# Delta rule: 64-step inverses from two blocks of 32 on 32x32 tiles of TensorE and a third from products; routing order and out-projection rewritten

## The chip, the cores and the metric

One core of one Trainium2 chip runs the whole program. The metric is the device time of one execution in microseconds, for fixed inputs. Everything is float32.

## The reference, cut to what matters

The program is one block of a bidirectional mixer model (neighbourhood attention, gated linear attention and a delta rule, whose outputs are concatenated and projected), followed by two layers of attention or a gated recurrence, each with a mixture of experts. 1024 tokens of width 1024 with 64 meta tokens ahead in the first block; 16 experts, each of which picks the 128 tokens it likes best.

```
# delta rule, per head (width 64) and per direction: state S, inputs r, decay w, k, v, a, b
S = S * w + (S @ a) b^T + v k^T ;  y = S @ r
# block one out
h = x + concat(o_na, o_gla, o_rw) @ w_out[0]
h = h * rsqrt(mean(h*h) + 1e-6) * final_norm_g
# expert choice
aff = softmax(x @ w_router);  gates, idx = top_k(aff^T, 128)
out[idx] += (silu(x[idx] @ gate) * (x[idx] @ up)) @ down * gates
```

The kernel computes the delta rule in chunks of 64 steps. Within a chunk it needs the inverse T = (I - A)^-1 of a unit triangular 64x64 matrix, A being strictly triangular. The doubling form is used: T = (I + A)(I + A^2)(I + A^4)..., for 64 steps up to A^32.

## The kernel before, in words

Each engine has its own instruction stream, written out by hand in Python (functions `..._tensor`, `..._vector`, `..._scalar`, `..._gpsimd`, and `sync` for the transfers), and each instruction waits for counters that the other engines' instructions raise. There is no planner: the order in each stream is the order of the calls.

**Delta rule** (`rwkv_branch`, 842 to 1612 us of the span). Eight heads are done as four pairs p of heads h = 0, 1. A pair has 17 chunks for each direction d = 0, 1. They are done in five groups: q = 0 with one chunk (the meta tokens), q = 1 to 4 with four chunks. A group G = 5p + q works in lane G % 2, which has three PSUM banks (`bank[0..2]`) and a strip of SBUF. So in a full group there are 2 heads x 4 chunks x 2 directions = 16 small problems side by side: direction d lies on partitions `B_(d)` (64 of them), the heads and chunks beside each other along the free axis. A product over a full group is 16 matmuls 64x64x64; as float32 each matmul gives two records (two passes) in the profile.

The steps of a group are: `scores_tensor` (A and the scores, masked by `masks_vector`), `powers_tensor` (A transposed, masked by `powers_vector`), `a_tensor`, `kb_tensor`, `v_turn_tensor` (transposes, copied by `front_scalar`), the levels, `akv_tensor`, `wu_tensor` (T times two right sides), `qpd_tensor` (matrices of the chunk's step), and `chain_tensor`, four dependent steps of the state.

A level e = 0 to 5 of the inverse (`level_tensor`, L1553 on) makes M = A^(2^(e+1)) in bank 0 (L1563, e < 5), its transpose MT in bank 1 (L1568, e < 4) and T's next term TT in bank 2 (L1578, e > 0). `m_scalar` (L1813) and `mt_scalar` (L1818) copy M and MT to SBUF on ScalarE, `mt1_vector` (L1981) copies the first MT on VectorE, `tt_vector` (L1986) adds the TT product to T on VectorE. GpSimd makes T = A + I at the start (`group_gpsimd`, L1354). So a full group has 5 + 4 + 5 = 14 level products.

TensorE's stream interleaves groups: levels 0, 1, 2 of G stand between level 5, akv, wu and qpd of G - 1; then come level 3 of G, scores and powers of G + 1 with chain steps of G - 1 between them, level 4 of G, and the transposes of G + 1. Between two pairs (`between_tensor`, and likewise on the other engines) the last group's levels 3 to 5, wu, qpd and chain stand among the wide projections of the next pair (L1402) and its low-rank products (L1423).

**Out-projection of block one** (`block_one_out`, 1612 to 1799.5). Eight tiles of 128 tokens. The SP queue loads the scale vector, the first tile's 12 source blocks (768 KB), a tile of x and then the weights in six transfers of 1 MB. `out_products` takes tile after tile: 12 blocks x 2 halves of 512 columns. VectorE adds x to both halves, ScalarE squares 1024 columns with a sum, VectorE scales and shifts, ScalarE takes the root, VectorE the reciprocal, and VectorE writes X.

**Routing** (`moe`, once per layer: 2285.5 to 2355.6 and 3566 to 3635.4). In turn k TensorE makes the logits of tile k - 1 (L3127), turns tile k of X (L3134), turns the logits of tile k - 1 (L3141), and spreads expert 0's column of tile k - 2 over a bank (L3108, `spread_tensor`). ScalarE copies X's transpose (L3228) and the logits (L3231), then takes the exponential of tile k - 1 (L3235). VectorE takes the maximum, normalizes (L3375, L3377), copies the transposed affinities (L3381) and counts, for each token of expert 0, how many are ahead of it (`count_vector`, L3324), reading the spread row from PSUM banks 6 and 7. Each spread waits until all counts of the tile before are done:

```
pe.wait_ge(counted.sem, counts_to[k - 2])
spread_tensor(pe, 0, k - 2)
```

When all 8 tiles are counted, the 128 tokens of expert 0 are listed (L3354, L3114), fetched by an indirect transfer and turned (L3160), and the experts' products begin (L3174), whose weights stream through a ring of 24 slabs of 512 KB.

The functions of the delta rule and the routing that the change touches, and their callers:

Of the kernel before, what the change touches and what calls it, by code (L numbers as in the profile page):

```python
# [13 lines left out]
P = 128  # L14
# [1171 lines left out]
def rwkv_branch(k, c, ps, io, hnT, mix, sb):  # L1186
# [5 lines left out]

    nc = k.nc
    with stage(k, sb) as st:
        PAIRS, GROUPS, FULL = 4, 5, 4
# [32 lines left out]
            "m_made", "m_copied", "mt_made", "mt1_copied", "mt_copied", "tt_made", "tt_added"))  # L1228
        akv_made, akv_copied, w_made, w_copied, u_made, u0_copied, u1_copied = (st.sem(n) for n in (
# [8 lines left out]
        class Lane:  # L1238


            def __init__(self, G):
# [11 lines left out]
                self.M, self.MT = (tall(0), tall(1)), (None, tall(4), tall(5), tall(4), tall(5))  # L1253
# [4 lines left out]
            def tall(self, i):  # L1258
                return self.bank[i][:, 0:2 * self.n * CH].rearrange("p (h c t) -> p h c t", h=2, t=CH)

# [65 lines left out]
        def prepare_gpsimd(gp, p):  # L1326
# [7 lines left out]
            for t in edges[0:4 if p else 8]:  # L1334
                gp.memset(t, 0.0).then_inc(*padded.up())
            for d, excl in enumerate((excl0, excl1)):
                gp.wait_ge(summed.sem, 3 * p + 1 + 2 * d)
                gp.tensor_tensor(excl, temps(p)[0][2 * d + 1], excl, ALU.subtract).then_inc(*excluded.up())
# [11 lines left out]
        def group_gpsimd(gp, G):  # L1350
            L = Lane(G)
            gp.wait_ge(masked.sem, 4 * G + 4)
            for d in range(2):
                gp.tensor_tensor(L.TT[B_(d)], L.SC[B_(d), d, :, :, sa],  # L1354
                                 eye[B_(d), :].unsqueeze(1).unsqueeze(1).broadcast_to([CH, 2, L.n, CH]),
                                 ALU.add).then_inc(*eyed.up())

        def gpsimd(gp):
            for p in range(PAIRS):
                prepare_gpsimd(gp, p)  # L1360
                for q in range(GROUPS):
                    group_gpsimd(gp, GROUPS * p + q)

# [179 lines left out]
        def m0_t(L, d, h, i):  # L1543
            return L.SC[B_(d), d, h, i, sa]

        def level_tensor(pe, G, e):
# [5 lines left out]
            else:  # L1552
                pe.wait_ge(m_copied.sem, 5 * G + e)  # L1553
                if e == 1:
                    pe.wait_ge(mt1_copied.sem, G + 1)
                elif e < 5:
                    pe.wait_ge(mt_copied.sem, 3 * G + e - 1)
            power = lambda d, h, i: L.M[e % 2][B_(d), h, i, :]
            power_t = lambda d, h, i: m0_t(L, d, h, i) if e == 0 else L.MT[e][B_(d), h, i, :]
# [5 lines left out]
            if e < 4:  # L1565
                for h, i in L.units():
                    for d in range(2):
                        x = pe.matmul(L.tall(1)[B_(d), h, i, :], power(d, h, i), power_t(d, h, i))  # L1568
                x.then_inc(*mt_made.up())
            if e:  # L1570
                if e == 1:
                    pe.wait_ge(eyed.sem, 2 * G + 2)
                    pe.wait_ge(akv_copied.sem, G + 1)
                else:
                    pe.wait_ge(tt_added.sem, 5 * G + e - 1)
                for h, i in L.units():
                    for d in range(2):
                        x = pe.matmul(L.tall(2)[B_(d), h, i, :], power(d, h, i), L.TT[B_(d), h, i, :])  # L1578
                x.then_inc(*tt_made.up())

# [73 lines left out]
        def between_tensor(pe, p):  # L1654

            G, old, new = GROUPS * p - 1, p > 0, p < PAIRS
            if old:
# [8 lines left out]
                chain_tensor(pe, G - 1, 2)  # L1666
            if new:
                k_tensor(pe, p, 0)
            if old:
                chain_tensor(pe, G - 1, 3)  # L1670
                level_tensor(pe, G, 5)
# [31 lines left out]
        def tensor(pe):  # L1703
            for i in range(2):
                block_tensor(pe, i, ps[3 * i:3 * i + 3], enumerate(SPANS))
            for p in range(PAIRS):
# [13 lines left out]
                for q in range(GROUPS):  # L1720
                    G = GROUPS * p + q
                    level_tensor(pe, G, 0)
                    if q:
                        level_tensor(pe, G - 1, 5)
# [31 lines left out]
                    if q >= 2:  # L1756
                        chain_tensor(pe, G - 1, 3)
                    v_turn_tensor(pe, G + 1)
# [51 lines left out]
        def m_scalar(ac, G, e):  # L1810
            L = Lane(G)
            ac.wait_ge(m_made.sem, 5 * G + e)
            ac.activation(L.M[e % 2], L.tall(0), ACT.Copy).then_inc(*m_copied.up())  # L1813

        def mt_scalar(ac, G, e):
            L = Lane(G)
            ac.wait_ge(mt_made.sem, 4 * G + e)
            ac.activation(L.MT[e], L.tall(1), ACT.Copy).then_inc(*mt_copied.up())  # L1818
# [1863 lines left out]
```

## Time and profile before

| | us |
|---|---|
| median of 3 runs | 4355.24 (4348.53 to 4356.75) |
| the profiled execution's own time | 4353.24 |
| its span | 4351.5 |
| TensorE busy (matmuls) | 4065.1 (93%) |
| VectorE, ScalarE, GpSimd busy | 1542.3, 1050.6, 288.7 |
| delta rule | 770, TensorE busy 726.9 |
| out-projection of block one | 187.5, TensorE busy 167.8 |
| routing, first and second layer | 70.1 and 69.4, TensorE busy 41.8 and 42.2 |

How to read it: the profile records every instruction of each engine. A matmul record's start is measured; its length contains the pipeline, so records of one product overlap and the distance of starts is what a product costs. "Idle before, releaser" is the time an engine stood still ahead of an instruction and whose semaphore ended it.

### The profile page before, as it was taken

To read this page: it belongs to the slowest core of one execution; us is meant where nothing else is said; L and a number is where in the kernel's file an instruction comes from. 1 tells how busy PE (TensorE), PEld (TensorE's weight loads), DVE (VectorE), ACT (ScalarE), POOL (GpSimd) and SP (SyncE) were. 2 spreads that over 40 slices of the span, in tenths; PEclk is the share of its full clock that TensorE was granted. 3 is DMA by queue.
4 is the path that set the end of the run, shared out by engine and by line. 5 is a ranking of instruction groups with operands and counts; after the bars stand their busy time and mean duration, and the time that the engine had idled before them with its cause. 6 is when DMAs were issued, how large, how long until landed. Compare 5 with 4: busy or idle time off the path is not lost. (4 is left out here: it accounts for less than half of the span.)

```text
span 4351.5 us, 65830 instructions
## 1 busy us (share of the span) xinstructions
PE 4065.1 (93%) x28648; PEld 2292.5 (53%) x28648; DVE 1542.3 (35%) x3438; ACT 1050.6 (24%) x2064; POOL 288.7 (7%) x350
## 2 busy tenths in 40 slices
PE   7999898999999979999997999999899887999998
PEld 4555575596868664554544444444444344444443
DVE  2344233435454531124655411112345627211113
ACT  2233221343333320104552000002234421000002
POOL 0000000101110100000110000000000110000000
PEclk9999899999999989999998999999999988999999
DMA  3000101100000013112007899998311126899997
GB/s 96 25 25 6 46 16 45 30 4 26 3 26 8 7 58 111 49 20 49 1 1 283 294 323 310 326 306 306 113 38 34 48 105 253 300 307 328 309 324 253
DMA packets 319470, 566.70 MB, mean 130 GB/s; under 512 B 47776, under 2 KB 127808, under 8 KB 319184
## 3 DMA queue, kind: packets, MB, share of 16 engines
q1 hardware_dynamic: 305296, 511.12, 34.7%
q0 software_dynamic: 9504, 34.61, 3.3%
q10 hardware_dynamic: 4384, 16.78, 1.0%
q8 instruction: 226, 3.70, 0.3%
q14 instruction: 60, 0.49, 0.0%
HBM read 514.20 MB, written 48.23 MB: 129 GB/s over the span
## 5 line engine op out<-in xcount | busy, mean ns | idle before, releaser
L3174 PE MATMUL bank<-ring,m_picked_T 128*128 128x512 f32 x2048 | 898.4, 597 | 4.1 <-ACT m_picked_T L3250 4.1
L3174 PEld LDWEIGHTS bank<-ring,m_picked_T 128*128 128x128 f32 x2048 | 389.3, 192 | 482.2 <-issue 476.6
L3174 PE MATMUL bank<-ring,m_hidden_T 128*128 128x512 f32 x1024 | 454.7, 592 | 0.0
L3174 PEld LDWEIGHTS bank<-ring,m_hidden_T 128*128 128x128 f32 x1024 | 189.8, 190 | 216.3 <-issue 216.3
L1402 PE MATMUL bank<-hnT,w_block 128*128 128x336 f32 (+3 forms) x800 | 270.9, 488 | 18.1 <-DMA w_block<-in_w_in 18.1
L376 PE MATMUL bank<-hnT,w_block 128*128 128x512 f32 (+3 forms) x640 | 248.2, 523 | 5.1 <-DMA w_block<-in_w_in 5.1
L3416 DVE TENSOR_TENSOR m_hidden<-m_hidden,bank 128x512 f32<-128x512 f32 x64 | 43.9, 686 | 522.0 <-ACT m_hidden L3256 522.0
L232 PE MATMUL bank<-xT,w_block 128*128 128x512 f32 x512 | 220.5, 592 | 1.0 <-DMA w_block<-in_lru_w_in 1.0
L1402 PEld LDWEIGHTS bank<-hnT,w_block 128*128 128x128 f32 x800 | 149.0, 192 | 106.6 <-issue 22.7
L2241 PE MATMUL bank<-out_w,out_in 128*128 128x512 f32 x384 | 167.8, 600 | 18.6 <-DMA out_w<-in_w_out 18.6
L3256 ACT ACTIVATE m_hidden<-bank 128x512 f32<-128x512 f32 x64 | 38.2, 597 | 540.1 <-PE bank L3174 540.0
L232 PEld LDWEIGHTS bank<-xT,w_block 128*128 128x128 f32 x512 | 97.2, 190 | 123.2 <-issue 122.0
L376 PEld LDWEIGHTS bank<-hnT,w_block 128*128 128x128 f32 x640 | 114.4, 192 | 77.7 <-issue 44.7
L2459 PE MATMUL bank<-xT,a_weights 128*128 128x512 f32 x320 | 140.5, 592 | 0.8 <-ACT xT L2340 0.8
L2241 PEld LDWEIGHTS bank<-out_w,out_in 128*128 128x128 f32 x384 | 74.0, 193 | 112.5 <-issue 112.5
L2814 PE MATMUL bank<-l_xc,l_wg 128*128 128x512 f32 x256 | 112.9, 602 | 19.4 <-ACT l_r L2880 17.0
L2520 PE MATMUL bank<-a_weights,xT 128*128 128x512 f32 x256 | 124.9, 615 | 0.4 <-ACT xT L2557 0.4
L3422 DVE COPY m_hidden_T<-bank 128x256 f32<-128x256 f32 x64 | 27.0, 422 | 273.9 <-PE bank L3167 273.9
L3547 POOL DMA_INDIRECT y_rows<-m_ys,m_tokens x30 | 47.7, 1589 | 1108.4 <-DVE m_ys L3431 1047.6
L3260 ACT ACTIVATE m_hidden_T<-bank 128x256 f32<-128x256 f32 x64 | 24.5, 383 | 393.3 <-PE bank L3167 393.3
L808 PE MATMUL bank<-hnT,w_block 128*128 128x512 f32 (+3 forms) x288 | 113.2, 550 | 0.0
L1986 DVE TENSOR_TENSOR rw_lane<-bank,rw_lane 128x512 f32<-128x512 f32 (+1 forms) x100 | 61.0, 610 | 145.1 <-PE bank L1578 145.1
(480 smaller groups left out, 5697.2 us busy)
## 6 DMA issues: line engine op xcount, KB each, us to landing
ring<-in_moe_w_gate_up SPq DMA_DIRECT2D x512, 512.0 KB, 7.6
ring<-in_moe_w_down SPq DMA_DIRECT2D x256, 512.0 KB, 4.6
w_block<-in_w_in SPq DMA_DIRECT2D x42, 512.0 KB, 3.8
x_rows<-X ACTq DMA_DIRECT2D x2, 4096.0 KB, 16.4
ring<-y_rows SPq DMA_DIRECT2D x16, 512.0 KB, 8.7
w_block<-in_lru_w_in SPq DMA_DIRECT2D x16, 512.0 KB, 3.9
out_in<-mix SPq DMA_DIRECT2D x8, 768.0 KB, 5.9
out_w<-in_w_out SPq DMA_DIRECT2D x6, 1024.0 KB, 13.4
```

The costliest lines, as they stand in the source:

```text
L232: m = pe.matmul(ps[banks + j][0:out_rows, 0:n], w[:, d, 0:out_rows], src[:, d, col:col + n], start=d == 0, stop=d == KD - 1)
L376: x = pe.matmul(bank_of(s + j)[:, 0:w], wb[b % RING][:, d, :], hnT[:, d, col:col + w], start=d == 0, stop=d == KD - 1)
L808: x = pe.matmul(bank(kind, p, j, h)[:, 0:n], wb[i % 3][:, d, :], hnT[:, d, col:col + n], start=d == 0, stop=d == KD - 1)
L1402: m = pe.matmul(banks[j][:, 0:n], wb[i % 3][:, d, :], hnT[:, d, col:col + n], start=d == 0, stop=d == KD - 1)
L1986: ve.tensor_tensor(L.part(2), L.bank[2][:, 0:2 * L.n * CH], L.part(2), ALU.add).then_inc(*tt_added.up())
L2241: m = pe.matmul(ps[2 * u + h][:, :], xt[u][:, b, :], wt[:, b, 512 * h:512 * h + 512], start=b == 0, stop=b == blocks - 1)
L2459: x = pe.matmul(ps[m % 4][:, :], w, xT[:, d, 512 * (m % 2):512 * (m % 2) + 512], start=d == 0, stop=d == KD - 1)
L2520: x = pe.matmul(ps[6 + half][:, :], oT[:, b, t * P:(t + 1) * P], weights[:, b, 512 * half:512 * half + 512], start=b == 0, stop=b == KD - 1)
L2814: out = pe.matmul(ps[s % 4][:, :], wg[:, q, z, h, x * P:(x + 1) * P], xc[:, h, col:col + w], start=h == 0, stop=h == 1)
L3174: m = pe.matmul(banks[j][:, :], lhsT[:, (i % 8) * P:(i % 8 + 1) * P], ring[:, i, j, :], start=i % 8 == 0, stop=i % 8 == KD - 1)
L3416: ve.tensor_tensor(hid[:, s], hid[:, s], ps[2 * h][:, :], ALU.mult).then_inc(*acted.up())
L3547: gp.indirect_dma_start(y_rows[:, :], bass.IndirectOffsetOnAxis(ap=tokens[:, e:e + 1], axis=0), ys[:, :], None, compute_op=ALU.add).then_i ...
```

## The change

**Delta rule.** A 64-step chunk is split into two blocks of HC = 32 steps. The diagonal blocks of T are inverted by doubling up to A^16, which needs one level less, on 32 of the partitions each, so that the two blocks of the two directions lie on four different 32x32 tiles of TensorE (`block(d, j)` gives the rows and columns of block j). A level product is now 32 matmuls 32x32x32 (64 records) in place of 16 of 64x64x64 (32 records); M is made in levels 0 to 3, MT in 0 to 2, TT in 1 to 4. The block off the diagonal is T2 * A21 * T1: `between_blocks_tensor` turns T1 ("back") and multiplies A21 with T2 ("cross"), ScalarE and VectorE copy the results, and `corner_tensor`, in the place of level 5, multiplies the two. GpSimd clears the zero corner of T and copies the diagonal blocks from their own tile TD to T (`place_gpsimd`); ScalarE and VectorE copy the corner. ScalarE's copies of v stand in a function of their own behind the copy of "back".

**Out-projection.** The first four tiles are done together, block by block: each block of weights (now 12 transfers of 512 KB on ScalarE's queue) and of sources (12 of 256 KB on SP's) is used as it lands. From tile 4 on it is tile after tile, one half after the other. The square is taken by halves, and the root by Ln and Exp.

**Routing.** In each turn ScalarE takes the exponential of tile k - 1 ahead of the logits' copy of tile k, and copies the spread row of tile k - 1 from PSUM to SBUF (`row0`); VectorE counts from there, and the spread waits for ScalarE's copy three turns back in place of the counts.

```
-        PAIRS, GROUPS, FULL = 4, 5, 4
+        PAIRS, GROUPS, FULL, HC = 4, 5, 4, 32
+            def block(self, d, j):
+                k = 1 - j if d and self.q else j
+                return slice(CH * (1 - d) + HC * k, CH * (1 - d) + HC * k + HC), slice(HC * k, HC * k + HC)
 # group_gpsimd, and behind it in the loop place_gpsimd of the group before
-                gp.tensor_tensor(L.TT[B_(d)], L.SC[B_(d), d, :, :, sa], eye..., ALU.add).then_inc(*eyed.up())
+                for j in range(2):
+                    rows, cols = L.block(d, j)
+                    gp.tensor_tensor(L.TD[rows], L.SC[rows, d, :, :, sa][:, :, :, cols],
+                                     eye[rows, cols].unsqueeze(1).unsqueeze(1).broadcast_to([HC, 2, L.n, HC]),
+                                     ALU.add).then_inc(*eyed.up())
+            for d in range(2):
+                gp.memset(L.TT[L.block(d, 1)[0]][:, :, :, L.block(d, 0)[1]], 0.0).then_inc(*tt_cleared.up())
+        def place_gpsimd(gp, G):
+            L = Lane(G)
+            gp.wait_ge(tt_added.sem, 4 * G + 4)
+            for d in range(2):
+                for j in range(2):
+                    rows, cols = L.block(d, j)
+                    gp.tensor_copy(L.TT[rows][:, :, :, cols], L.TD[rows]).then_inc(*tt_placed.up())
+            gp.wait_ge(*tt_placed.now())
 # level_tensor
-            if e < 5:
-                for h, i in L.units():
-                    for d in range(2):
-                        x = pe.matmul(L.tall(0)[B_(d), h, i, :], power_t(d, h, i), power(d, h, i))
+            blocks = [(h, i, d, j) for h, i in L.units() for d in range(2) for j in range(2)]
+            if e < 4:
+                for h, i, d, j in blocks:
+                    x = pe.matmul(L.half(0)[L.block(d, j)[0], h, i, :], power_t(h, i, d, j), power(h, i, d, j))
 ...
+        def between_blocks_tensor(pe, G):
+            pe.wait_ge(tt_added.sem, 4 * G + 4)
+            for h, i in L.units():
+                for d in range(2):
+                    first = L.block(d, 0)[0]
+                    x = pe.matmul(L.half(1)[side(d), h, i, :], L.TD[first, h, i, :], c["ident"][first, first])
+            x.then_inc(*back_made.up())
+            for h, i in L.units():
+                for d in range(2):
+                    second = L.block(d, 1)[0]
+                    x = pe.matmul(L.half(0)[side(d), h, i, :], L.M[0][second, h, i, L.block(d, 0)[1]], L.TD[second, h, i, :])
+            x.then_inc(*cross_made.up())
+        def corner_tensor(pe, G):
+            pe.wait_ge(back_copied.sem, G + 1)
+            pe.wait_ge(cross_copied.sem, G + 1)
+            for h, i in L.units():
+                for d in range(2):
+                    x = pe.matmul(L.half(2)[L.block(d, 0)[0], h, i, :], L.back[side(d), h, i, :], L.cross[side(d), h, i, :])
+            x.then_inc(*corner_made.up())
 # wu_tensor
-            pe.wait_ge(tt_added.sem, 5 * G + 5)
+            pe.wait_ge(tt_placed.sem, 4 * G + 4)
+            pe.wait_ge(tt_cleared.sem, 2 * G + 2)
+            pe.wait_ge(corner0.sem, G + 1)
+            pe.wait_ge(corner1.sem, G + 1)
 # tensor, in the loop over q
-                        level_tensor(pe, G - 1, 5)
+                        corner_tensor(pe, G - 1)
 ...
                     if q >= 2:
                         chain_tensor(pe, G - 1, 3)
+                    between_blocks_tensor(pe, G)
                     v_turn_tensor(pe, G + 1)
 # block_one_out
+            for b in range(BLOCKS):
+                pe.wait_ge(mix_in[b].sem, 16)
+                pe.wait_ge(w_in[b].sem, 16)
+                for t in range(TOGETHER):
+                    for h in range(2):
+                        m = product(t, h, b)
 # moe, tensor
-                    else:
-                        pe.wait_ge(counted.sem, counts_to[k - 2])
+                    elif k >= 4:
+                        pe.wait_ge(row_in.sem, k - 3)
 # moe, scalar: the exponential stands ahead of the logits' copy, and at the end of a turn
+                if k >= 1:
+                    ac.wait_ge(spread[0].sem, k)
+                    ac.activation(row0[:, (k - 1) * P:k * P], spread_bank(0, k - 1), ACT.Copy).then_inc(*row_in.up())
```

## Rows read from the trace of the kernel before

**Rows 1.** The page's engines, stretches by stage (busy per engine), the instruction queue.

```profile
PE 4065.1 (93%) x28648; PEld 2292.5 (53%) x28648; DVE 1542.3 (35%) x3438; ACT 1050.6 (24%) x2064; POOL 288.7 (7%) x350
...
842.00:1612.00 770.00, 726.92 (x15011) 579.40 (x15009) 366.33 (x665) 262.34 (x471) 88.72 (x79) 0.99 0.04 12
1612.00:1799.50 187.50, 167.80 (x384) 73.96 (x384) 23.77 (x41) 12.10 (x25) 0.00 (x0) 0.95 0.29 95
2285.50:2355.60 70.10, 41.78 (x251) 31.09 (x251) 35.72 (x210) 14.63 (x44) 1.47 (x4) 0.74 0.66 248
...
q8 instruction: 226, 3.70, 0.3%
```

**Rows 2.** Stretches: one steady group of the delta rule, columns as before.

```profile
911.97:940.27 28.30, 27.75 (x856) 26.48 (x852) 13.07 (x29) 9.43 (x17) 2.53 (x2) 1.00 0.01 3
```

**Rows 3.** TensorE in order of time inside that group: start, length, line, idle before.

```profile
914.76 1.16 PE L1500 MATMUL bank<-rw_ar,rw_kb 64*128 64x128 f32 x16 [0.49 <-DVE rw_lane L1967]
...
916.83 1.10 PE L1563 MATMUL bank<-rw_lane 64*64 64x64 f32 x32
917.76 1.10 PE L1578 MATMUL bank<-rw_lane 64*64 64x64 f32 x32
918.70 0.40 PE L1648 MATMUL bank<-rw_state,rw_lane 64*64 64x64 f32 x8
918.93 0.40 PE L1651 MATMUL bank<-rw_lane,rw_state 64*64 64x64 f32 x8
919.26 1.09 PE L1522 MATMUL bank<-ident,rw_ar 128*64 128x128 f32 x16
...
922.57 1.15 PE L1563 MATMUL bank<-rw_lane 64*64 64x64 f32 x32
923.55 1.10 PE L1568 MATMUL bank<-rw_lane 64*64 64x64 f32 x32
```

**Rows 4.** TensorE in order of time where akv meets level 1; four short records.

```profile
926.06 0.22 PE L1563 MATMUL bank<-rw_lane 64*64 64x64 f32 x1
926.07 0.22 PE L1586 MATMUL bank<-rw_lane 64*64 64x64 f32 x1
...
926.13 0.28 PE L1563 MATMUL bank<-rw_lane 64*64 64x64 f32 x3
...
322.79 0.24 PE L425 MATMUL bank<-na_k,na_q 64*64 64x16 f32 x4
```

**Rows 5.** VectorE and GpSimd in order of time, steady group and between two pairs.

```profile
909.38 0.76 DVE L2005 TENSOR_TENSOR rw_lane<-bank,rw_dec 128x256 f32<-128x256 f32 x2 [1.13 <-PE bank L1630]
...
917.77 0.47 DVE L2021 SCALAR_TENSOR_TENSOR rw_state<-bank,rw_dec,rw_lane 128x64 f32<-128x64 f32 x2
...
917.34 2.61 POOL L1354 TENSOR_TENSOR rw_lane<-rw_lane,rw_eye 64x512 f32<-64x512 f32 x2 [24.47 <-DVE rw_lane L1967]
...
1202.73 0.76 DVE L1997 TENSOR_TENSOR rw_lane<-bank,rw_ar 128x256 f32<-128x256 f32 x2 [5.65 <-PE bank L1609]
```

**Rows 6.** Out-projection in order of time, and a transfer of 512 KB.

```profile
1615.44 0.33 SPq L2265 DMA_DIRECT2D final_g<-in_final_norm_g  x1
...
1626.60 23.60 PE L2241 MATMUL bank<-out_w,out_in 128*128 128x512 f32 x48 [18.63 <-DMA out_w<-in_w_out]
...
1764.63 29.77 PE L2241 MATMUL bank<-out_w,out_in 128*128 128x512 f32 x69
...
1794.44 1.29 DVE L2285 TENSOR_TENSOR h_tile<-bank,h_in 128x512 f32<-128x512 f32 x2 [16.19 <-PE bank L2241]
...
w_block<-in_w_in SPq DMA_DIRECT2D x42, 512.0 KB, 3.8
```

**Rows 7.** Routing in order of time, TensorE and ScalarE.

```profile
2307.04 1.09 PE L3134 MATMUL bank<-ident,X 128*128 128x128 f32 x8 [1.25 <-DVE m_aff L3381]
...
2333.14 0.45 PE L3108 MATMUL bank<-ident,m_aff_tiles 128*128 128x128 f32 x1 [3.60 <-DVE m_junk L3324]
...
2305.82 0.27 ACT L3231 ACTIVATE m_logits<-bank 16x128 f32<-16x128 f32 x1 [2.09 <-PE bank L3127]
```

More of the change, by code:

```diff
@@ L1571, in level_tensor, with side @@
                 if e == 1:
-                    pe.wait_ge(eyed.sem, 2 * G + 2)
+                    pe.wait_ge(eyed.sem, 4 * G + 4)
                     pe.wait_ge(akv_copied.sem, G + 1)
                 else:
[L1575 to L1578, printed above, removed]
+                    pe.wait_ge(tt_added.sem, 4 * G + e - 1)
+                for h, i, d, j in blocks:
+                    rows = L.block(d, j)[0]
+                    x = pe.matmul(L.half(2)[rows, h, i, :], power(h, i, d, j), L.TD[rows, h, i, :])
                 x.then_inc(*tt_made.up())
+        def side(d):
+            return slice(HC * (1 - d), HC * (1 - d) + HC)
+        def between_blocks_tensor(pe, G):
+            L = Lane(G)
+            pe.wait_ge(tt_added.sem, 4 * G + 4)
[10 more added lines that the diff above has]
+        def corner_tensor(pe, G):
+            L = Lane(G)
+            pe.wait_ge(back_copied.sem, G + 1)
[4 more added lines that the diff above has]
+            x.then_inc(*corner_made.up())
         def akv_tensor(pe, G):
@@ L2269, in sync, with product @@
                     "(k p) e -> p k e", p=P)).then_inc(*k.router_in.up(16))
+            for t in range(TOGETHER, NT):
+                if t >= TOGETHER + 2:
+                    sp.wait_ge(made.sem, 2 * (t - 1))
+                sp.dma_start(xt[t % 2][:, :, :],
+                             mix[0:BLOCKS, :, t * P:(t + 1) * P].rearrange("b p t -> p b t")).then_inc(*src_in[t % 2].up(16))
+                x_tile(t)
             sp.wait_ge(*k.router_in.now())
         def tensor(pe):
-            out_products(pe, ps, blocks, wt, xt, src_in, w_in, used, taken)
+            def product(t, h, b):
+                src = first[:, b, t * P:(t + 1) * P] if t < TOGETHER else xt[t % 2][:, b, :]
+                return pe.matmul(ps[2 * (t % 4) + h][:, :], src, wt[:, b, 512 * h:512 * h + 512], start=b == 0,
+                                 stop=b == BLOCKS - 1)
@@ new lines, in tensor @@
+            for b in range(BLOCKS):
+                pe.wait_ge(mix_in[b].sem, 16)
[3 more added lines that the diff above has]
+                        m = product(t, h, b)
+                        if b == BLOCKS - 1:
+                            m.then_inc(*made.up())
+            for t in range(TOGETHER, NT):
+                pe.wait_ge(src_in[t % 2].sem, 16 * (t // 2 - 1))
+                for h in range(2):
+                    pe.wait_ge(added.sem, 2 * (t - 4) + h + 1)
+                    for b in range(BLOCKS):
+                        m = product(t, h, b)
+                    m.then_inc(*made.up())
@@ L2302, in block_one_out @@
+                ac.wait_ge(totalled.sem, t + 1)
+                ac.activation(s[:, 2:3], s[:, 2:3], ACT.Ln, bias=eps[:, :], scale=1.0 / D).then_inc(*logged.up())
+                ac.wait_ge(*logged.now())
+                ac.activation(s[:, 3:4], s[:, 2:3], ACT.Exp, scale=-0.5).then_inc(*rooted.up())
+        nc.gpsimd.memset(eps[:, :], 1e-6).then_inc(*eps_set.up())
         sync(nc.sync)
         tensor(nc.tensor)
+        scalar(nc.scalar)
         vector(nc.vector)
-        scalar(nc.scalar)
@@ L3103, in spread_bank @@
         def spread_bank(x, t):
-            return ps[(6, 2)[x] + t // 4][:, t % 4 * P:t % 4 * P + P]
+            return ps[2 + t // 4][:, t % 4 * P:t % 4 * P + P] if x else ps[6 + t % 2][:, 0:P]
         def spread_tensor(pe, x, t):
@@ L3323, in count_vector @@
                 ve.wait_ge(counted.sem, counted.n - 3)
+            row = ps[2 + first // 4][:, first % 4 * P:first % 4 * P + n * P] if x else row0[:, first * P:last * P]
             ve.scalar_tensor_tensor(junk[counted.n % 4][:, 0:n * P].rearrange("p (k j) -> p k j", j=P),
-                                    ps[(6, 2)[x] + first // 4][:, first % 4 * P:first % 4 * P + n * P].rearrange(
-                                        "p (k j) -> p k j", j=P), aff[:, t, x:x + 1],
+                                    row.rearrange("p (k j) -> p k j", j=P), aff[:, t, x:x + 1],
                                     weight[:, :].unsqueeze(1).broadcast_to([P, n, P]), op, ALU.mult,
@@ L3381, in vector @@
                     ve.tensor_copy(affT[:, t * P:t * P + P], ps[2 * (t % 3)][0:NE, 0:P]).then_inc(*aff_taken.up())
-                    ve.wait_ge(spread[0].sem, t + 1)
+                    ve.wait_ge(row_in.sem, t + 1)
                     count_before_vector(ve, 0, t)
```

179 lines of the change are left out of this document (116 added, 63 removed).

## Prediction

> **What bounds the kernel now.** First the share of busy time by engine and by stage [rows 1]: TensorE works 4065 of 4351.5 us. The change touches four places. In the delta rule (842 to 1612 us) TensorE is busy 726.9 of 770 us, VectorE 366, ScalarE 262. The out-projection (1612 to 1799.5) is TensorE's too, with 18.6 us of wait ahead of it. In the routing of the first expert layer (2285.5 to 2355.6; the second is alike) it is busy 60% and waits for VectorE. Then one steady group of the delta rule [rows 2]: it repeats every 28.30 us, TensorE busy in 27.75, VectorE in 13.1, ScalarE in 9.4, GpSimd in 2.5. So in a group TensorE's time is the time. The order of its instructions [rows 3] shows no gap but 0.49 us for a mask.
>
> **What one product costs.** A product over a full group is 16 matmuls, 32 records. L1563 starts at 916.83, L1578 at 917.76: 0.93 us, or 58 ns for each round of two records, one in each of two 64x64 tiles [rows 3]. In L2241 69 records of 512 columns take 29.77 us; without the last one's 0.60 that is 0.429 us each, 0.84 ns a column [rows 6]. 64 columns are 53 ns, so a round carries 5 ns besides. The new product is 32 matmuls of 32 columns, 64 records on four tiles. If four run side by side, a round is 27 + 5 = 32 ns, and 16 rounds take 0.51 us. That four can run side by side is seen where L1586 (off the diagonal) meets L1563 (on it): seven starts between 926.06 and 926.13, of which the first two and the last group stand in [rows 4], so four different tiles share one round of 58 ns. No row has 32x32 tiles. From below: four records of 16 columns end 0.24 us after the first starts and last 0.19, so two rounds start within 0.05, about 29 ns a round, 0.46 us a product [rows 4]. From above: if only two records share a round of 32 ns, 32 rounds, 1.01 us. I take 0.51, since the row nearest in kind shows four tiles. The three off-diagonal products (back, cross, corner: 32 records on two tiles) are 16 rounds too, 0.51 each.
>
> **A change of tile form.** From 64x64 to 128x64, L1651's eight records from 918.93 would be through at 919.16, the next form starts at 919.26: 0.10. The first product after a change (922.57 to 923.55) takes 0.98, not 0.93: 0.05 more [rows 3]. I price each new change at 0.15 us; bounds 0 and 0.3 (twice the row). That 32x32 after 64x64 is such a change no row shows; if it is none, the delta rule is 17 x 0.9 = 15 us better than below. The Trainium skill (TensorEngine Tiling (Array Packing), Key Properties) lists 32x32 and 64x64 as different modes and says that a change of mode, not of tile, drains the engine.
>
> **A steady group (q = 2, 3), step by step.** L0: two products, 1.86 to 1.02: +0.84. Level 5 (0.93) becomes the corner (0.51): +0.42. L1 and L2: three products each, 2.79 to 1.53: +1.26 twice. L3: M, MT, TT become M, TT: 2.79 to 1.02: +1.77. Back and cross are new: -1.02. L4: M and TT (1.86) become TT (0.51), but chain step 2 behind it waits for VectorE, which does two masks, the inverse mask and chain step 1 until 918.24 [rows 5]. From the start of scores 1 (914.76) that is 3.48, with 0.06 to the start 3.54, where chain 2 now starts at 3.94: only +0.40. New form changes around akv (2), wu (2), ahead of qpd, ahead of back: 6 x 0.15 = -0.90; those around L4 lie in the wait. Sum: 4.0 us, the group 24.3. Nothing else comes late: scores wait for ds_ready, on which VectorE works 0.76 us behind L1630 [rows 5], while L3 lasts 1.02. The new copies on ScalarE and VectorE are half as wide and lie beside a, kb, v_turn and akv. On GpSimd the identity adds are four of 32 partitions in place of two of 64 at 1.3 us [rows 5]; with two memsets and four copies I put 5.6 us behind the mask. wu's turn comes 10.6 us behind it (1.0 to chain 2, then 9.6 by the steps above), so it is hidden; if every such operation took 1.3 us it would be 11.
>
> **The rest of the pair.** Group q = 1 has no chain and a small corner: 3.7. Group q = 4 has L0 to L2 and corner: 0.84 + 0.42 + 2.52 - 0.75 = 3.0. Its L3, L4, back, cross and corner lie between pairs among wide projections; there VectorE waits for TensorE (5.65 us before L1997 [rows 5]), so it counts: 1.77 + 1.35 - 1.02 + 0.42 - 5 x 0.15 = 1.8. Group q = 0 has a quarter of the records and waits for copies: 0.5, bounds -1 and 2. Sum 0.5 + 3.7 + 4.0 + 4.0 + 3.0 + 1.8 = 17.0, four pairs: **68 us**. Bounds, for 17 groups' worth (16 full ones and four quarters): a round of 29 ns shortens 12.5 product lengths by 0.05 us each, 11 us, so 79; products of 1.01 us cost 0.5 on each of ten (the eleventh, L4's, lies in the chain's wait), 85 us, so -17.
>
> **Out-projection.** The stage's first transfer is issued at 1615.44, the first product starts at 1626.60 [rows 6]: 11.2 us for 768 KB of source, 1 MB of scale and x, and 1 MB of weights. After: 256 KB of source on one queue and 512 KB of weights on another, which is behind a table load. 512 KB land in 3.8 us [rows 6]; both pieces land in 3.8 if they don't hinder each other, in 5.7 if they come one after the other; I take 4.6, and 1.7 for the table and the issue: 6.3 us, so 4.9 less; bounds 0 and 7. Later blocks are hidden: at most 5.7 us of transfer beside 8 matmuls, 6.9 us. The 192 products stay. Behind the last one VectorE now adds both halves (1.29 [rows 6]); then one of them lies under the last half's products: 0.7, bounds -0.5 (two squares, one operation more) and 1.5. Sum **5.6 us**.
>
> **Routing.** The transposes of a turn wait 1.25 us for m_aff, which hangs on the exponential of the tile before, and that stands on ScalarE behind the logits copy [rows 7]; six turns are alike. With the exponential ahead of it the wait goes. But ScalarE then waits for the spread row, which TensorE makes behind the transposes, and copies it, before it copies X: by my count the logits start 0.9 later in a turn. Net 0.35 a turn, 2 us. More is in the last turns, where the spread waits for all counts of the tile before: 3.60 us [rows 7], and the next one about as much. Behind row_in it doesn't wait, and VectorE, whose own work these counts are, loses only the hand-over from TensorE and ScalarE: I take 5 of the 7.5. **7 us**, bounds 2 (the turns alone) and 10 (all of it). Choice, list, gather and the first expert's products hang on the last count in line, so it arrives whole, and in both layers: **14 us**. The experts behind are TensorE's and unchanged.
>
> **Sum.** 68 + 5.6 + 14 = 88. The profiled execution took 4353.2 (span 4351.5), 2.0 under the median of the three runs, 4355.2, and within their spread. Against the median: 4355 - 88 = **4267 us**.
>
> **Rivals.** (a) Two tiles, not four, share a round: product 1.01, the delta rule gives -17 (above): 4355 + 17 - 20 = 4352, no change. For it: every diagonal product of this trace runs two. Against: the starts of [rows 4]. 5%. (b) The other side: TensorE starts small records no faster than one in about 29 ns, as it now does on average. Then 64 records are 1.86 us, a full group gains 11 x 1.86 + 3 x 0.93 + 0.90 - 13.0 = 11.1, 17 groups 189 us: 4355 + 189 - 20 = 4524. It decides from a product of 0.93 us, 14 ns a record. Against: starts 1 to 10 ns apart [rows 4]. The Trainium skill (TensorE: Matmul & The Clock Gate, Wait — 56ns, not 53.3ns?) says that start to start never drops below about 25 ns however small N is; as a limit of the whole engine that would be 1.6 us a product and, as an estimate by that page, 4470. The trace agrees with it for a single tile only (29 ns a round). 5%. (c) Program fetch: 3.70 MB of instructions came in 226 packets [rows 1]; at 8 records and loads in 32 ns the products use 4 ns an instruction, 3.6 times the present rate. If feeding held them to 0.6 us a product: +20, 4287. 6%. (d) GpSimd's placing or a wait inside q = 0 and the last stage stands in line, 1 us a group: 4284. 6%. My forecast 78%.
>
> **How the numbers follow.** Range 4248 to 4308: below by 0.46 us a product (11) and half the form changes free (8); above by 0.6 us a product (19), form changes at 0.3 (15) and half of the routing's gain (7). It takes in (c) and (d), and leaves (a), (b) and a tenth of the rest out. A measurement can tell 0.2%, 8.7 us. Faster 0.90 (forecast, c, d), same 0.05 (a), slower 0.05 (b).
>
> **What would show it.** Right: a group period of 24 to 25 us; level products of x64 records starting 0.5 apart; chain 2 waiting about 0.7 us for VectorE's rw_state; wu with no wait for GpSimd; L3134's wait for m_aff gone and the counts' end 50 us after the stage's start, not 57; the first out product 6 to 7 us after its stage starts. Wrong: level products 0.9 us or more apart (a, b); a gap before L2's products with no releaser (c); wu waiting for POOL (d).

## The result, and the profile after

The changed kernel takes 4447.4 us (median of 4 runs, 4446.0 to 4458.3) against 4356.0 for the kernel before beside it: ratio 1.0218, 95% interval 1.0197 to 1.0239. I had forecast 4267, range 4248 to 4308. It is slower by 91 us where I said faster by 88, and the time lies outside the range. The profiled execution took 4446.0, span 4444.2.

First the page of the changed kernel: its engines, TensorE's instruction queue, and one of its groups of instructions. They answer to [rows 1].

```profile
PE 4057.8 (91%) x34632; PEld 2274.3 (51%) x34632; DVE 1523.7 (34%) x3450; ACT 1028.1 (23%) x2104; POOL 340.1 (8%) x511
...
q8 instruction: 273, 4.47, 0.4%
...
L1618 PE MATMUL bank<-rw_lane 32*32 32x32 f32 x4352 | 64.9, 206 | 36.5 <-issue 36.5
```

Then the stretches of the same kernel: the delta rule, the out-projection, the first routing, and one steady group (span; PE, PEld, DVE, ACT, POOL busy; clock; DMA share; GB/s).

```profile
842.00:1729.00 887.00, 732.52 (x20995) 566.70 (x20993) 344.86 (x679) 230.69 (x469) 139.97 (x239) 0.90 0.04 11
1729.00:1912.50 183.50, 166.68 (x385) 73.59 (x385) 26.63 (x38) 18.06 (x52) 0.17 (x2) 0.96 0.28 98
2398.20:2461.70 63.50, 39.61 (x251) 30.31 (x251) 35.96 (x210) 16.35 (x52) 1.42 (x4) 0.77 0.73 273
...
927.69:963.02 35.33, 28.13 (x1201) 25.61 (x1200) 11.96 (x30) 7.70 (x16) 5.05 (x10) 0.90 0.02 4
```

This steady group takes 35.3 us, not 24.3, and TensorE stands still in 7.2 of them; before it stood still in 0.5 of 28.3 [rows 2]. TensorE is busy 28.1 us, 0.4 more than before, at a mean clock of 0.90 of 2.4 GHz (1.00 before). Stage by stage, from the first transfer or product of a stage to that of the next: the delta rule +121.3 us (the out-projection's first transfer is issued at 1736.71, before at 1615.44), the out-projection -8.4, the first routing -6.6, the second -12.8. That sums to 93.5, and the span grew by 92.7. So the small parts gained what was forecast and more, and the delta rule alone lost it.

Where does TensorE wait in the delta rule? The waits of that stretch (engine, line, releaser: us in total, times, longest):

```profile
PE bank L1618 <- issue: 36.5, 21, 2.5
PE bank L1608 <- issue: 26.1, 23, 2.3
PE bank L1604 <- issue: 10.7, 10, 1.6
PE bank L1666 <- issue: 10.4, 6, 2.3
PE bank L1537 <- DVE rw_gate L2254: 8.0, 4, 2.0
```

"issue" means that the profile shows no semaphore that held it. L1604, L1608 and L1618 are the level products M, MT and TT, L1646 the corner, L1666 wu. All waits on "issue" of TensorE in the stage sum to 111 us; before there were none. Its other waits, nearly all for VectorE like the last line, sum to 41 us, and were 35 before. GpSimd is named nowhere. In order of time, TensorE in one stretch of a steady group (start, length, line, idle before):

```profile
905.20 0.66 PE L1646 MATMUL bank<-rw_lane 32*32 32x32 f32 x29 [1.37 <-issue]
905.78 1.15 PE L1654 MATMUL bank<-rw_lane 64*64 64x64 f32 x32
906.86 0.72 PE L1604 MATMUL bank<-rw_lane 32*32 32x32 f32 x62
...
908.65 0.73 PE L1608 MATMUL bank<-rw_lane 32*32 32x32 f32 x62 [1.02 <-issue]
909.23 0.74 PE L1618 MATMUL bank<-rw_lane 32*32 32x32 f32 x64
909.94 0.24 PE L1666 MATMUL bank<-rw_lane 64*64 64x64 f32 x1
912.45 3.38 PE L1666 MATMUL bank<-rw_lane 64*64 64x64 f32 x63 [2.27 <-issue]
```

Two things are to be seen. A gap can fall in the middle of a product whose waits were all met: one record of L1666 runs, the next 63 come 2.3 us later. And a product that no gap meets is fast: L1608 to L1618 is 0.58 us, 128 records and loads in all, where the 64 of a 64x64 product took 0.93 [rows 3].

The gaps end in steps of 3.4 to 3.8 us: 905.20, 908.65, 912.45. Here is what the DMA engines moved from 903 to 928 us, in 40 slices of 0.625 us; nothing but seven packets of TensorE's instruction queue, 16 KB each:

```profile
GB/s 26 0 0 0 0 26 0 0 0 0 26 0 0 0 0 0 26 0 0 0 0 0 26 0 0 0 0 0 26 0 0 0 0 0 0 26 0 0 0 0
```

A packet of 16 KB holds 256 instructions, 64 bytes each: the stage has 42,317 instructions of TensorE (41,985 records and loads, and the instructions on semaphores) and 165 packets, 256.5 each. I numbered TensorE's instructions through the whole program, in order of time. 78 gaps, 112 us of them together, stand at the same number modulo 256 (193), and nearly all end 1.2 to 1.6 us after a packet has landed. Call a packet starved when TensorE waited so for its first instruction. From the start of the packet before to the start of a starved one lie 3.57 us (median; 3.07 to 3.87 from the 10th to the 90th in a hundred), whatever products stand between, and 3.84 where the one before was starved too (41 times). So **TensorE waited for its own program**: 256 instructions take about 3.5 us to be replaced, 13.7 ns each, and level products on four 32x32 tiles use up 256 in 1.1 us. A steady group has 2412 instructions now, 9.4 packets, 33.6 us at 3.57 each and 36.2 at 3.84; the eight steady periods took 34.2 to 38.9. Before it had 1708, 6.7 packets, 24 us, below the 28.3 that the work takes.

The Trainium skill (Advanced Engine Details and Errata, ISA Cache) says that a cache line for instructions holds 256 of them and that there are only two. The places of the gaps agree with the 256. The same list gives TensorE 128 KB, which would be eight such lines; the 446 instructions that a stream below had in store when it began fit two lines and not eight. The section gives no time for a refill; the 3.5 us are this trace's.

The second thing that changed is the clock. In the stage, TensorE ran at 1.2 GHz in 27 stretches that sum to 180.5 us; before in 3, of 13.6 us together. One of them is the 3.38 us of L1666 above: 63 records in 3.3 us, two 64x64 tiles side by side, 107 ns a round (one record on each tile) and not 58.

### The profile page after: what moved, and what is told of

The parts are those of the page before. It is cut to its first block and busy times, and to the rows that moved or that the text cites. A ratio compares the mean times of both kernels' runs of the same rounds, so it can differ in the third digit from the quotient of the medians.

```text
span 4444.2 us, 78122 instructions
## 1 busy us (share of the span) xinstructions
PE 4057.8 (91%) x34632; PEld 2274.3 (51%) x34632; DVE 1523.7 (34%) x3450; ACT 1028.1 (23%) x2104; POOL 340.1 (8%) x511
## 5 line engine op out<-in xcount | busy, mean ns | idle before, releaser
L2978 PE MATMUL bank<-xT,l_gT 128*128 128x512 f32 x256 | 110.1, 593 | 0.8 <-ACT l_i L3026 0.8
L2605 PEld LDWEIGHTS bank<-xT,a_weights 128*128 128x128 f32 x320 | 60.7, 190 | 76.7 <-issue 75.6
L1618 PE MATMUL bank<-rw_lane 32*32 32x32 f32 x4352 | 64.9, 206 | 36.5 <-issue 36.5
```

Source lines behind the costliest of these rows:

```text
L1618: x = pe.matmul(L.half(2)[rows, h, i, :], power(h, i, d, j), L.TD[rows, h, i, :])
L2605: x = pe.matmul(ps[m % 4][:, :], w, xT[:, d, 512 * (m % 2):512 * (m % 2) + 512], start=d == 0, stop=d == KD - 1)
L2978: out = pe.matmul(ps[2 * (t % 4) + h][:, :], gT[:, b, t * P:(t + 1) * P], wo[:, b, 512 * h:512 * h + 512], start=b == 0, stop=b == KD - 1)
```

## The experiments

Theory F says that the supply of instructions is the loss. The rivals named in the expectations are R (the other parts of the change cost something), T (tile forms or their changes make the gaps), S (TensorE itself needs 14.5 ns an instruction) and C (TensorE's own time at the low clock sets the group).

**The parts apart.** `rwkv_branch` of the kernel before in the changed kernel:

```
-def rwkv_branch(...):   # 32-blocks
+def rwkv_branch(...):   # as before the change
```

> The changed kernel with the delta rule of the kernel before (64x64 tiles, six levels), so only the new out-projection and the new routing are left of the change. Theory F (the whole loss is in the delta rule, where TensorE's instructions arrive too slowly): about 4328 us, as the stretches of the changed kernel's trace say (out-projection -8, routing -6.6 and about -13). Rival R (the new out-projection or routing shifts transfers and costs part of the loss): above 4340.

Measured 4328.9 us, ratio 0.9944 (0.9928 to 0.9961); again in five rounds 4327.0, 0.9939 (0.9926 to 0.9951). The out-projection and both routings gain 25 and 27 us together in these two comparisons, close to the 27.8 of the stretches, and R is out: all of the loss is in the delta rule.

**Twice the instructions on 64x64 tiles.**

```
-  x = pe.matmul(L.tall(0)[B_(d), h, i, :], power_t(d, h, i), power(d, h, i))
+  for s in (slice(0, 32), slice(32, 64)):      # both directions inside, for each s
+      x = pe.matmul(L.tall(0)[B_(d), h, i, s], power_t(d, h, i), power(d, h, i)[:, s])
```

> The kernel before, each level product of 64 columns issued as two matmuls of 32 columns on the same 64x64 tile: the same arithmetic and the same tiles, forms, waits and copies, but 128 instructions a product in place of 64; no 32x32 tile anywhere. Theory F (a packet of 256 instructions takes about 3.6 us to be replaced, however little the engine does in it): a steady group has 2604 records and loads in place of 1708, 10.2 packets, at 3.6 to 3.75 us each 36 to 38 us in place of 28.3, and the whole kernel about 4500 us (4470 to 4530). Rival T (the gaps come from the change between 32x32 and 64x64 tiles, or from four tiles at once): only the longer rounds count, 0.09 us a product, 14 products, 17 groups: 4377 us, and no gap without a releaser.

Measured 4563.9, ratio 1.0482 (1.0463 to 1.0501): near neither number, and this one is a miss of mine. TensorE in order of time:

```profile
1002.40 2.02 PE L1564 MATMUL bank<-rw_lane 64*64 64x32 f32 x64
1004.24 2.04 PE L1570 MATMUL bank<-rw_lane 64*64 64x32 f32 x64
```

A product takes 1.84 us: with 32 columns a round costs as much as with 64, about 58 ns. The engine was slow enough for its instructions (256 in 3.7 us), and there was no gap at a packet. The experiment says nothing against F, but it does not show it either: F and S fit it alike. (The clock stayed at 1.00 in the stage, with 32 columns in every level product.)

**Half the instructions, all the forms.** Only the first diagonal block's level products are made; the second block's are left out, so the result is not the reference's:

```
-  blocks = [... for d in range(2) for j in range(2)]
+  blocks = [... for d in range(2) for j in range(1)]
```

> The changed kernel without the level products of the second diagonal block (left out: M, MT and TT of that block, its copies are scaled by zero). Every tile form, change of form, wait and copy stays, and a product still is 16 rounds, but of 64 instructions in place of 128. Theory F: a steady group has 1708 records and loads, 6.7 packets, 24 us at 3.6 each, so the group is bound by both about equally and takes 25 to 27 us; the kernel 4270 to 4320 us. Rival T (changes of form, placing on GpSimd or the waits make the gaps): they are all still there, so the gaps stay and the kernel is above 4400.

Measured 4325.7, ratio 0.9941 (0.9922 to 0.9960), 6 us over the end of F's range and 74 under T's bound. The gaps at packet boundaries fell from 78 (112 us) to 24 (20 us); tile forms, their changes and the waits were all there. The order of TensorE:

```profile
957.01 0.80 PE L1673 MATMUL bank<-rw_lane 64*64 64x64 f32 x20 [0.93 <-issue]
957.74 0.69 PE L1611 MATMUL bank<-rw_lane 32*32 32x32 f32 x32
958.27 0.67 PE L1615 MATMUL bank<-rw_lane 32*32 32x32 f32 x32
958.78 0.67 PE L1625 MATMUL bank<-rw_lane 32*32 32x32 f32 x32
959.38 0.56 PE L1687 MATMUL bank<-rw_lane 64*64 64x64 f32 x11
```

Products start 0.51 to 0.53 apart, and 0.60 where the form changes. But the clock did not come back with the gaps: 15 stretches at 1.2 GHz, 140 us. The longest ones lie where groups q = 0 and 1 are worked on, and hold hardly any gap; most of this one's time goes to products on larger tiles:

```profile
1284.00:1301.00 17.00, 15.84 (x289) 14.01 (x291) 5.76 (x14) 1.94 (x4) 3.92 (x8) 0.50 0.01 3
```

So the low clock is not only a consequence of waiting for instructions. It can have cost this kernel up to 63 us (half of 140 - 13.6), which would be enough to explain why it is level with the old delta rule (4328.9) although its products are short; no run separates it.

**Tiles of 64 rows x 32 columns.** The kernel before, 128 instructions a product, 64 columns moved by each, and no 32-row tile:

```
-  x = pe.matmul(L.tall(0)[B_(d), h, i, :], power_t(d, h, i), power(d, h, i))
+  for j in range(2):
+      x = pe.matmul(L.tall(0)[quarter(d, j), h, i, :], power_t(d, h, i)[:, side(j)], power(d, h, i))
```

> The kernel before, each level product issued as tiles of 64 rows x 32 columns: two matmuls of 64 moving columns for one, on four tiles, so the arithmetic, the copies and (by the trace so far) the 0.93 us of array time a product stay, but a product has 128 instructions. No 32-row tile and no 32-column operand. Theory F (256 instructions take about 3.6 us to be replaced): a steady group has 2604 records and loads, 10.2 packets, 36 to 38 us in place of 28.3; gaps without a releaser, each starting at the same place modulo 256 instructions; the kernel 4460 to 4530 us. Rival S (an instruction costs TensorE itself 14.5 ns in 64-row tiles, as the doubled products of the run before would also fit): products of 1.86 us without gaps, 4564 us. Rival T (gaps belong to 32x32 tiles and their changes): 4355 us.

Measured 4499.2, ratio 1.0338 (1.0321 to 1.0356), inside F's range, 65 under S and 144 over T. TensorE in order of time:

```profile
912.38 1.78 PE L1600 MATMUL bank<-rw_lane 64*64 64x64 f32 x53 [1.26 <-issue]
914.09 1.10 PE L1566 MATMUL bank<-rw_lane 64*32 64x64 f32 x64
915.01 0.38 PE L1572 MATMUL bank<-rw_lane 64*32 64x64 f32 x10
916.11 0.92 PE L1572 MATMUL bank<-rw_lane 64*32 64x64 f32 x51 [0.72 <-issue]
```

L1566 to L1572 is 0.92 us, the array time of before, with twice the records: S is out. 93 gaps of 98 us lie at one place modulo 256 instructions, 3.48 us apart in the median where starved, and low clock is rare (7 stretches, 27 us). So the loss comes without 32x32 tiles and at full clock: the part of T that lays it to them is out. A change of form (64x32 to 64x64) is still there; the streams below have none. The kernel lost 145 us, 98 of them in gaps: a starved packet costs more than its gap.

**More work in the same instructions.** The changed kernel, each level product moving its 32 columns twice:

```
-  x = pe.matmul(L.half(0)[L.block(d, j)[0], h, i, :], power_t(h, i, d, j), power(h, i, d, j))
+  x = pe.matmul(both(0, h, i, d, j), power_t(h, i, d, j), twice(power(h, i, d, j)))
```

> The changed kernel with every level product moving its 32 columns twice (the second copy goes to unused columns of the bank and is not read): 64 columns a record, the same number of instructions, waits and copies. It adds about 0.42 us of array time to each of 11 products, 4.6 us a steady group. Theory F: the added work lies in the time that the engine spends waiting for instructions; the kernel stays at 4447 us within 25, and the gaps without a releaser shrink from 112 us to under 60. Rival C (TensorE's own time, at its low clock, sets the group): 17 groups of 4.6 us more, 4525 us.

Measured 4439.3, ratio 1.0203 (1.0186 to 1.0220), not to be told from the changed kernel's 1.0218 (1.0197 to 1.0239). Some 4 us of array time more in a group (a product starts 0.92 behind the one before in place of 0.54), 70 us in 17 groups, cost nothing, where C said 4525. The gaps at packet boundaries shrank only to 85 us, not under 60 as I had written: much of the added time was paid by the clock, which stayed up (9 stretches at 1.2 GHz, 41 us, against 27 and 180.5). That gives back up to half of 139.5, 70 us as well. So this run by itself does not show that the low clock costs the changed kernel nothing. As the whole cause C is out by other numbers: TensorE ran nothing in the 112 us of the gaps, and the narrow kernel above lost more with its clock up.

```profile
914.86 1.10 PE L1625 MATMUL bank<-rw_lane 32*32 32x64 f32 x64
917.31 0.68 PE L1687 MATMUL bank<-rw_lane 64*64 64x64 f32 x16 [1.36 <-issue]
```

**The supply by itself.** Streams of matmuls on zeros with pauses between them:

```
+for i in range(512):
+    for d in range(4):
+        h = slice(32 * d, 32 * d + 32)
+        pe.matmul(ps[...][h, 32 cols], a[h, 32 cols], a[h, 0:32])      # L3809; L3826 beside loads
```

> Only streams of matmuls on zeros, nothing of the reference is computed: 512 pairs on two 64x64 tiles with 64 columns, the same with 32 columns, 512 x 4 on four 32x32 tiles with 32 columns, 256 x 4 with 128 columns, and the 512 x 4 again beside a queue of 512 KB loads. Theory F: the 64x64 streams run at 58 ns a round, 3.7 us for 256 instructions, without gaps; the 32x32 stream with 32 columns (8192 instructions, 32 packets) runs in bursts of 1.1 us and takes 3.6 us a packet, 115 us in all, against some 35 us of work; with 128 columns (4096 instructions, 16 packets, about 55 us of work) 58 us; beside the loads longer than 115. Rival T (gaps come from changes of tile form): 35 us without gaps for the 32x32 stream.

It computes nothing of the reference and was run once. TensorE's order of time, with its waits, in the streams of 32x32 tiles; L3826 is the one beside the loads:

```profile
276.96 3.20 PE L3809 MATMUL bank<-blocks 32*32 32x32 f32 x223 [15.25 <-DVE res L3781]
281.55 1.27 PE L3809 MATMUL bank<-blocks 32*32 32x32 f32 x128 [1.38 <-issue]
285.28 1.93 PE L3809 MATMUL bank<-blocks 32*32 32x32 f32 x128 [2.46 <-issue]
288.73 1.93 PE L3809 MATMUL bank<-blocks 32*32 32x32 f32 x128 [1.52 <-issue]
...
405.33 58.63 PE L3816 MATMUL bank<-blocks 32*32 32x128 f32 x2048 [15.28 <-DVE res L3781]
...
572.42 1.93 PE L3826 MATMUL bank<-blocks 32*32 32x32 f32 x128 [4.29 <-issue]
578.63 1.93 PE L3826 MATMUL bank<-blocks 32*32 32x32 f32 x128 [4.29 <-issue]
```

And the stretches of the streams: 64x64 with 64 columns, 64x64 with 32, 32x32 with 32, 32x32 with 128, 32x32 with 32 beside loads.

```profile
75.30:137.00 61.70, 61.70 (x2048) 61.57 (x2048) 0.00 (x0) 0.00 (x0) 0.97 0.02 4
152.30:261.70 109.40, 109.40 (x2048) 109.27 (x2048) 0.00 (x0) 0.00 (x0) 0.50 0.01 2
277.00:390.00 113.00, 60.93 (x4096) 56.83 (x4096) 0.00 (x0) 0.00 (x0) 0.52 0.02 4
405.30:464.00 58.70, 58.63 (x2048) 57.73 (x2048) 0.00 (x0) 0.00 (x0) 0.96 0.02 4
552.70:693.80 141.10, 61.64 (x4096) 57.49 (x4096) 0.00 (x0) 0.00 (x0) 0.50 0.46 182
```

In the third stream there is one tile form, no semaphore inside and no other engine: bursts of 128 records (with their loads 256 instructions), 3.46 us from one to the next in 17 of 30 cases, 3.73 in 11 and 4.0 in two, all 31 gaps exactly 256 instructions apart; 113 us where F said 115 and T 35. T is out, as to changes of form too. The spacing did not hang on the engine's speed: the clock fell behind the second row (bursts of 1.27 us became 1.93; 0.52 over the stream), and the bursts still came every 3.46 to 3.73. The first burst is 446 instructions long, and its last record started before a packet landed: so many were held when it began. With 128 columns the same tiles run 58.6 us without a gap: 256 instructions of work in 3.66 us are just enough. Beside the loads a packet takes 6.21 us, and 3.46 again when they are over.

**A version for both gains.** The powers are masked to their diagonal blocks once, behind level 0, and kept as 64x64 matrices; T's blocks are stacked, 32 columns:

```
-  ve.tensor_copy(L.MT[1], L.half(1))
+  ve.tensor_tensor(part, bank, m_diag, ALU.mult)                    # M and MT of level 0, on VectorE
-  x = pe.matmul(L.half(2)[rows, h, i, :], power(h, i, d, j), L.TD[rows, h, i, :])
+  x = pe.matmul(L.half(2)[B_(d), h, i, :], power(d, h, i), L.TD[B_(d), h, i, :])
```

> A version meant to keep both gains: the changed kernel with the powers kept as block-diagonal 64x64 matrices (masked once, behind level 0), so M and MT are products of 64x64 tiles with 64 columns as before, and TT is one of 64x64 tiles with the 32 columns of the stacked blocks. 64 instructions a product throughout, five levels. Theory F: 1708 records and loads a group, TensorE's work about 26 us, some windows of 256 instructions still under 3.6 us: a group of 26.5 to 28, the kernel 4290 to 4325 us. Rival T (gaps from changes between 32-column and 64-column forms): above 4340.

Measured 4324.1, ratio 0.9935 (0.9919 to 0.9952). In more rounds:

> The block-diagonal version again, in more rounds, to be told from the next: 4324 us, 0.1% under the old delta rule with the new stages.

> The old delta rule with the new out-projection and routing again, in more rounds: 4329 us.

4325.9, ratio 0.9936 (0.9923 to 0.9949), against 4327.0, 0.9939 (0.9926 to 0.9951), for the old delta rule with the new stages. The first number is at the upper end of F's range and under T's bound. Both versions beat both kernels, by 0.6% the kernel before; which of the two is faster these runs can't tell, so next to all of the gain is that of the out-projection and the routings. No packet starves, the clock is 0.99 in the stage, and a steady group is 28.0 us. By the products' lengths (no run tests it) it is not 26.5 because TT's 32 columns on 64x64 tiles take 0.90 us in place of 0.93, which is what the doubled kernel showed of such products.

**Two products on 32x32 tiles.** In that version TT of levels 3 and 4 alone:

> The block-diagonal version, with the products TT of levels 3 and 4 alone on 32x32 tiles (128 instructions, 0.55 us, in place of 64 and 0.90). These two stand where TensorE's instructions are longest (scores, chain, projections between pairs). Theory F with the turnaround read so far (3.5 us for 256 instructions): a steady group has 1836 records and loads, 7.2 packets, 25.1 us at the least, so few windows starve; 0.35 us less on one product a group (the other lies in the chain's wait for VectorE) and on two between pairs: 4324 - 8 = 4316 us, 4308 to 4324. If windows around level 3 starve after all: gaps of 1 us there, 17 of them, 4335 us.

Measured 4329.3, ratio 0.9946 (0.9934 to 0.9958): no gain over 0.9936 (0.9923 to 0.9949), and my 4316 missed. Steady groups took 27.8 to 28.9 us. Nine packets starved, 4.9 us in all, none for more than 1.2; that takes up part of the 8 us which the shorter products were to bring, and the rest is open.

## Why the prediction was wrong, point by point

- **The step that failed** is the first conclusion, "So in a group TensorE's time is the time", and with it the price of rival (c), "If feeding held them to 0.6 us a product: +20, 4287." It took for granted that instructions come as fast as short products use them, and they don't: TensorE stood still for 112 us at packet boundaries. I saw that the products use 4 ns an instruction, 3.6 times the rate of before, and chose 0.6 us without asking the trace how fast instructions can come. At 13.7 ns an instruction a product of 128 can't average under 1.75 us in a run of such products. Its chance of 6% was the chance of the mechanism that happened, and its sign, a gap with no releaser, came; its price should have been: 9.4 packets x 3.5 = 33 us a steady group, +4.7 over before for each of 17, so 4355 + 80 - 20 = 4415 at least.
- The number was in the trace of before: packets of 16 KB in the delta rule were never closer than 3.33 us, and 62 of 117 spacings were under 4.25. The supply was near its limit already, though nothing starved; four level products of 0.93 are 256 instructions in 3.72 us.
- **Product of 0.51 us**: right. 0.58 with 64 records on four tiles, 0.51 to 0.53 with 32 on two, and back 0.41. Four tiles do share a round (rival a is out), and records start every 9 ns within a burst (rival b is out as it was put, as a limit of TensorE itself; but where packets starve the supply sets 13.7 ns an instruction, 27 ns a record with its load, nearly b's 29).
- **Change of form 0.15**: too dear. 0.60 in place of 0.51 to 0.53, so some 0.08.
- **A steady group 24.3**: as TensorE's time at full clock it is about right: with half the instructions four of the eight steady periods took 24.8 to 25.5 us, starved packets among them (one in the rows above), and the other four 26.4 to 28.4. The saving of 68 us is not shown by any run as a whole, since the clock was down too in the runs on 32x32 tiles of 32 columns, which I had not thought of: 140 us at half speed in that run against 13.6 before.
- **GpSimd and VectorE**: right. wu never waits for GpSimd; chain 2 waits 0.54 us for rw_state, where I wrote about 0.7.
- **Out-projection 5.6**: 8.4. The start was better than priced: 4.8 us from the first transfer to the first product in place of 11.2, I had 6.3; the tail 0.9, I had 0.7; products 1.1.
- **Routing 7 a layer**: 6.6 in the first, 12.8 in the second. m_aff's wait is gone and a turn went from 5.08 to 4.78 us (0.30, I had 0.35). In the second layer of before, five turns of logits ran 3.10 to 3.58 us in place of 1.91, at a granted clock of 0.51 to 0.60, and in the first layer one (3.28); after none did. That is 7.7 us in the second layer and 1.4 in the first. Without them each layer's gain is 5.1 to 5.2 us, under the 7 forecast; that the sum came out above it is luck, since I had forecast nothing of the clock. (Counted from its first product the second layer's routing took 75.5 us before; the 69.4 of the table ahead begin 6.1 us later.)

For the last two points, one of the five slow turns of the kernel before, in its second layer, and then the changed kernel's rows in order of time: the start of the out-projection, VectorE's last sum in it, a turn of the routing and the last spreads.

```profile
3598.24 3.58 PE L3127 MATMUL bank<-m_spare,router 128*16 128x128 f32 x16
...
1736.71 6.42 SPq L2374 DMA_DIRECT2D out_first<-mix  x12
...
1741.53 4.00 PE L2392 MATMUL bank<-out_w,out_first 128*128 128x512 f32 x5 [12.65 <-DMA out_w<-in_w_out]
...
1908.22 0.69 DVE L2421 TENSOR_TENSOR h_tile<-bank,h_in 128x512 f32<-128x512 f32 x1 [9.55 <-PE bank L2392]
...
2431.61 1.91 PE L3274 MATMUL bank<-m_spare,router 128*16 128x128 f32 x16 [1.33 <-ACT m_spare L3375]
...
2444.83 1.97 PE L3255 MATMUL bank<-ident,m_aff_tiles 128*128 128x128 f32 x8 [2.95 <-DVE m_aff L3533]
```

The latter answer to [rows 6] and [rows 7]: both halves of the last sum were 1.29 us behind the last product, now one of 0.69; and the last spread starts 46.6 us after the stage's first product, where it was 53.2.

Of the 189 us between the measured +121.3 and the forecast -68, the gaps at packet boundaries are 112. How the other 77 are shared is open; two readings of the traces give their size. First the clock: 60 of the 180 us at 1.2 GHz lie in packets whose successor starved, where a faster engine would, by F, only have waited longer, and 117 in the others, where they can have cost half at most, 59 us (3 before). Then what a starved packet costs beside its gap: in the narrow kernel, 145 less 98 of gaps and at most 7 for the clock leaves 40 us over 93 starved packets, so as an estimate at most 33 us for the 78 here. The wide kernel fits both: its gaps are 27 us shorter and its clock is up, and the added work took the place of both.

## What to carry to other kernels

Count TensorE's instructions, not only its busy time: records and loads in a stretch, divided by 256, times the closest spacing of its instruction packets in the trace. Where that nears the stretch's time, a change that does the same work in more and smaller matmuls makes it slower, however well the tiles overlap. A gap with no releaser that falls inside a product, a multiple of 256 instructions behind the last one, is the mark of it.

## What the runs showed of the hardware

- TensorE's instructions come in packets of 256, about 3.5 us apiece and in the delta rule never less than 3.2 apart in any run (3.46 the most common in the stream); beside a queue of 512 KB loads 6.21 us.
- On 64x64 tiles a record of 32 columns costs what one of 64 does, about 58 ns a round (1.84 us for 64 records in two tiles, no gap); on 32x32 tiles a round of such records costs 32 to 36 ns (0.51 to 0.58 us for 16 rounds).
- Clock: the stream of 64x64 tiles with 32 columns was busy 109.40 of 109.40 us and stayed at 1.2 GHz throughout, coming from a stream at 0.97 and a pause; the one with 64 columns ran at 0.97. In the delta rule with half the products, 15.84 of 17 us busy went by at 1.2 GHz. So a low clock can stand beside an engine that never idles. What brings it is not shown: level products of 32 columns on 64x64 tiles left the stage at 1.00 (doubled), level products of 64 columns on 32x32 tiles had 41 us at 1.2 GHz (wide), and the narrow kernel had 27 us in spite of 98 us of gaps.
